# Streaming the rows of the projections' products backwards through TensorE

## The reference

```python
# first model, each of 2 layers, T = 272
proj = rms_norm(h, norm_mix_g[l]) @ w_in[l]                 # 1024 -> 2560
q, k, v, xr, gate = jnp.split(proj, splits, axis=-1)
h = h + jnp.concatenate([o_attn, o_rec], axis=-1) @ w_out[l]  # attention and a recurrence
g, u = jnp.split(rms_norm(h, norm_ffn_g[l]) @ w_gu[l], [D_FF], axis=-1)
h = h + (jax.nn.silu(g) * u) @ w_down[l]                    # 2816 -> 1024

# second model, each of 2 layers, T = 512 and 256
y, yc = even_mixer(xm, cm, w_in_ab, ...)  # layer 0: x @ w_in, gated MLP, windowed attention, @ w_out
y = odd_mixer(xm, cm, w_qkv_c, ...)       # layer 1: x @ w_qkv, attention, @ w_out
h = h + gt_m * rms_norm_2(y, g_post_m)
f = conv_ffn(modulate(h, ...), w_up[layer], conv_w[layer], conv_b[layer], w_down[layer])
h = h + gt_f * rms_norm_2(f, g_post_f)
```

## Time and profile before

| | |
|---|---|
| time, median of 3 runs | 1695.95 us (1694.21 to 1696.47) |
| the profiled execution | 1696.95 us |
| its span, first to last instruction | 1695.1 us |
| matmuls on TensorE | 11870, busy 1622.8 us (96%) |
| VectorE, ScalarE busy | 1017.2 us (60%), 869.4 us (51%) |
| moved by DMA | 253.94 MB, mean 150 GB/s |

### The profile page before, as it was taken

How to read it: one execution, slowest core, us unless ns; L and a number is a source line. 1 busy time by engine, 2 the same in 40 slices (tenths; PEclk the granted TensorE clock), 3 DMA queues, 4 the chain that set the end, 5 groups by cost and what they waited for, 6 DMA issues and landing times.

```text
span 1695.1 us, 28191 instructions
## 1 busy us (share of the span) xinstructions
PE 1622.8 (96%) x11870; PEld 1419.8 (84%) x11870; DVE 1017.2 (60%) x1577; ACT 869.4 (51%) x1467; POOL 21.1 (1%) x38
## 2 busy tenths in 40 slices
PE   6999999999999999999989999999999898999997
PEld 6968999989789999987757778888888674789997
DVE  7675545465756455724464765425556877687675
ACT  6764534448555444534565553323444647665563
POOL 0000000000000000310000000000000000000000
PEclk9999999999899999999999999999999999999999
DMA  7465445353556464772201553232223530254642
GB/s 297 140 248 210 159 156 200 138 193 139 199 190 233 141 232 142 208 242 82 75 1 56 182 207 104 84 126 100 84 69 112 207 114 26 76 217 150 218 145 91
DMA packets 60525, 253.94 MB, mean 150 GB/s; under 512 B 4977, under 2 KB 8305, under 8 KB 42481
## 3 DMA queue, kind: packets, MB, share of 16 engines
q1 hardware_dynamic: 59088, 249.01, 41.3%
q0 software_dynamic: 1312, 3.15, 1.0%
HBM read 251.09 MB, written 1.05 MB: 149 GB/s over the span
## 4 chain that ended last, share of the span: by engine, by line
PE 82%; DVE 9%; ACT 6%; issue 2%; DMA 0%; SPq 0%; DVEq 0%; ACTq 0%
PE PA L916 63%; PE PA L976 4%; DVE WL_t L1571 2%; PE PB L851 2%; PE PB L1339 2%; PE PA L1004 2%; ACT WH_t L2298 1%; PE PB L1326 1%; PE PA L953 1%; PE PA L958 1%; PE PA L952 1%; PE PA L871 1%; PE PB L1269 1%; ACT tmp L2741 1%; DVE Y L1953 1%
## 5 line engine op out<-in xcount | busy, mean ns | idle before, releaser
L916 PE MATMUL PA<-XH_t,WH_t 128*128 128x256 f32 (+2 forms) x1984 | 628.1, 317 | 3.7 <-DVE WL_t L1571 1.5
L1571 DVE TENSOR_TENSOR WL_t<-raw,WH_t 128x1024 fp32r<-128x1024 f32 (+1 forms) x344 | 444.5, 1297 | 307.2 <-ACT WH_t L2298 306.8
L916 PE MATMUL PA<-XL_t,WH_t 128*128 128x256 f32 (+2 forms) x1984 | 622.8, 314 | 0.0
L916 PE MATMUL PA<-XH_t,WL_t 128*128 128x256 f32 (+2 forms) x1984 | 622.6, 314 | 0.0
L2298 ACT ACTIVATE WH_t<-raw 128x1024 fp32r<-128x1024 f32 (+1 forms) x344 | 380.8, 1111 | 158.8 <-PE PA L916 139.6
L916 PEld LDWEIGHTS PA<-XH_t,WH_t 128*128 128x128 f32 x1984 | 375.8, 189 | 34.2 <-issue 6.0
L916 PEld LDWEIGHTS PA<-XH_t,WL_t 128*128 128x128 f32 x1984 | 375.8, 189 | 21.4
L916 PEld LDWEIGHTS PA<-XL_t,WH_t 128*128 128x128 f32 x1984 | 375.9, 189 | 21.3 <-issue 0.5
L916 PE MATMUL PA<-AH_t,WH_t 128*128 128x256 f32 (+2 forms) x616 | 192.0, 312 | 0.3 <-DVE AL_t L1617 0.2
L916 PE MATMUL PA<-AH_t,WL_t 128*128 128x256 f32 (+2 forms) x616 | 190.9, 310 | 0.0
L916 PE MATMUL PA<-AL_t,WH_t 128*128 128x256 f32 (+2 forms) x616 | 190.3, 309 | 0.0
(11 more groups left out here) (281 smaller groups left out, 1723.8 us busy)
## 6 DMA issues: line engine op xcount, KB each, us to landing
raw<-in_w_ada SPq DMA_DIRECT2D x48, 1024.0 KB, 5.0
raw<-in_w_gu SPq DMA_DIRECT2D x44, 1024.0 KB, 4.8
raw<-in_w_dn SPq DMA_DIRECT2D x64, 704.0 KB, 4.1
raw<-in_w_up SPq DMA_DIRECT2D x44, 1024.0 KB, 4.8
raw<-in_w_in SPq DMA_DIRECT2D x30, 1024.0 KB, 5.7
raw<-in_w_out SPq DMA_DIRECT2D x12, 1024.0 KB, 4.8
raw<-in_w_qkv SPq DMA_DIRECT2D x6, 1024.0 KB, 6.1
raw<-in_w_outc SPq DMA_DIRECT2D x4, 1024.0 KB, 4.8
```

What stands on the lines that cost most here:

```text
L916: mm = pe.matmul(PA[:, (L.b0 + o) % 4, 0:T], W[:, c:c + P], X[:, k, L.x0:L.x0 + T], start=(n == 0 and m == 0 and not L.early), stop=(n == ...
L1571: dve.tensor_tensor(WL_t[:, w:w + L.cols], RAWV[:, r % RAW, part * UNIT:part * UNIT + L.cols], WHf[:, w:w + L.cols], ALU.subtract).then_in ...
```

## The change

A helper `back` turns the order of columns of a view round: it starts at the last column and steps by -1. It is put around the PSUM operand and the moving operand of every product of the projections, at the five places named above. The same columns are multiplied and the same sums land in the same places; the order in which TensorE walks along a row is reversed. Weights, waits, signals, banks and the order of the products are as before.

```diff
+            def back(t):
+                return t[:, ::-1]
...
-                        pe.matmul(PA[:, (L.b0 + o) % 4, 0:L.T], W[:, c:c + P], X[:, k, L.x0:L.x0 + L.T],
+                        pe.matmul(back(PA[:, (L.b0 + o) % 4, 0:L.T]), W[:, c:c + P], back(X[:, k, L.x0:L.x0 + L.T]),
...
-                                mm = pe.matmul(PA[:, (L.b0 + o) % 4, 0:T], W[:, c:c + P], X[:, k, L.x0:L.x0 + T],
+                                mm = pe.matmul(back(PA[:, (L.b0 + o) % 4, 0:T]), W[:, c:c + P], back(X[:, k, L.x0:L.x0 + T]),
...
-                    pe.matmul(PA[:, bank, 0:L.T], WH_t[:, c:c + P], hi[:, k, 0:L.T], start=(k == 0), stop=False)
-                    pe.matmul(PA[:, bank, 0:L.T], WH_t[:, c:c + P], lo[:, k, 0:L.T], start=False, stop=False)
+                    pe.matmul(back(PA[:, bank, 0:L.T]), WH_t[:, c:c + P], back(hi[:, k, 0:L.T]), start=(k == 0), stop=False)
+                    pe.matmul(back(PA[:, bank, 0:L.T]), WH_t[:, c:c + P], back(lo[:, k, 0:L.T]), start=False, stop=False)
...
-                            pe.matmul(PA[:, bank % 4, a:b], WH_t[:, c:c + P], x[:, k, a:b], start=(k == 0 and x is hi),
+                            pe.matmul(back(PA[:, bank % 4, a:b]), WH_t[:, c:c + P], back(x[:, k, a:b]), start=(k == 0 and x is hi),
...
-                            mm = pe.matmul(PA[:, bank % 4, a:b], WL_t[:, c:c + P], hi[:, k, a:b], start=False,
+                            mm = pe.matmul(back(PA[:, bank % 4, a:b]), WL_t[:, c:c + P], back(hi[:, k, a:b]), start=False,
```

More of the change, by code:

```diff
@@ L957, in second_down @@
                     c = w + k * P
-                    mm = pe.matmul(PA[:, bank, 0:L.T], WL_t[:, c:c + P], hi[:, k, 0:L.T], start=False, stop=(k == FH - 1))
+                    mm = pe.matmul(back(PA[:, bank, 0:L.T]), WL_t[:, c:c + P], back(hi[:, k, 0:L.T]), start=False, stop=(k == FH - 1))
                 mm.then_inc(S("out_ready"), 1)
```

## The result

| | before | after |
|---|---|---|
| median of 4 runs | 1696.21 us (1694.21 to 1698.05) | 1704.34 us (1702.74 to 1704.61) |
| ratio to before | | 1.0047, 95% interval 1.0035 to 1.0059 |
| span of the profiled execution | 1695.1 us | 1702.8 us |

A forecast was written before the change was run, and what follows sets the result against it. PE's list of matmuls was taken to bound the kernel. With 0 per column, 0 per product and 0 elsewhere, the profiled 1696.95 us stayed, 1696.0 us against the median; the range was 1690 to 1724 us.

The forecast's parts named there:

- What bounds the kernel: Whole kernel: PE is busy 1622.8 of 1695.1 us; the touched 9024 products hold it for 1331 us, 78% of the span.
- Price per column, 0: Touched products, 2,906,880 columns: a backward step costs between 0 and +0.422 ns a column; 0 was taken.
- the half rate: Rival, touched products: a backward row loses the pairing of neighbours, +0.422 ns a column, 1227 us, giving 2924 us; chance 0.14.
- The two rows taken as evidence: L1021's moving row cut in runs of 64 and L1143's step-0 weight read: neither slower than ordinary, speaking for 0 per column.
- Same within 0.2%: Whole kernel: time changes by no more than about 3.4 us, following from the no-difference case; chance 0.72.
- The 0.72: Whole kernel: chance given to no difference, the likeliest case, at 1696.0 us.
- And their pattern isn't touched. So nothing outside the two patterns gets a price: Weight loads of 128 columns, 189 ns each, run under the products unchanged; everything outside the moving and PSUM patterns: 0 us.
- The split in 0.422 ns a column and 11.4 ns fixed: Touched products' pace, from 119.4 ns at 256 columns and 227.4 at 512: a cost per column plus a fixed part per product.
- The start cost: Rival, touched products: starting a backward row costs 1 to 3 ns each, 9 to 27 us, giving 1705 to 1724 us; chance 0.08.
- start on the same boundaries: Touched rows: seen from the other end, even widths and the 16-token offset keep neighbours paired, so cost per product was taken as 0.
- Less fixed cost: Rival, touched products: the fixed 11.4 ns shrinks by 1 ns (1688 us) up to all of it (1594 us); chance 0.06.
- PSUM: Sums in PSUM: each column is revisited after the same 119 to 227 ns and readers wait as before; 0 us.

## Why the prediction was right or wrong

**What bounds the kernel: right.** All of the 7.7 us appeared as busy time of PE; counts of products and columns held, and so did the leverage: 9.0 us for each nanosecond per product.

**Price per column, 0: right against the half rate, wrong as a form.** No product came near 0.84 ns a column; the upper end of 1227 us was not there. The two rows taken as evidence pointed the right way on that. But they are single means of few products, those of the earlier trace rows are durations with the way through the pipe and no paces, and they could not show 1 or 2%, which is the size of all that happened here (6.2 ns of 227.1). "Same within 0.2%" asked for a pace right to 0.4 ns per product, and no row of the trace bounds a change of the read pattern that tightly. The 0.72 was too high for that reason alone. That the time is within the range owes something to luck: 12.5 us lost at 512 columns and 5.7 us won at the other widths, by the ledger, stand behind the small sum, and the prediction had neither.

**"And their pattern isn't touched. So nothing outside the two patterns gets a price": this is the step that failed.** The weight loads run under the products and the chain never names them, yet a load's reads meet the row's. Moving the weights by 16 columns, with everything else as it was, took a 256-column product from 120.0 to 113.3 ns. The Trainium skill says in "TensorE: Matmul & The Clock Gate" (Step-by-step: what each phase is for) that PE has two read ports of its own, and that loading the next weights takes nothing from the running matmul's read bandwidth. The prediction priced the loads as if this held. The measured 6.7 ns speak against it for this pace, and they decide.

**The split in 0.422 ns a column and 11.4 ns fixed: a fit through two points, not a law.** Forwards the part beyond columns / 2.4 is 58 ns at 128 columns, 13.2 at 256, 10.0 at 264, 11.9 at 272, 13.3 at 384, 16.1 at 448. The check at 272 columns agreed within a nanosecond (126.2 against 126.7), but the effect in question is of that size, and the same kernel's other rhythm gives 125.3 there.

**The rivals.** The start cost forecast 1705 to 1724 us and the time came within a microsecond of it, but its mechanism is wrong: +6.2, -0.8 and -1.6 ns at three widths are no start cost. That the time lay near is no merit of that rival. (Its lower end is counted from the median and its upper from the profiled execution, 1 us apart.) The sentence that all rows "start on the same boundaries" looked at the row alone; the boundary that counts is the distance to the weights. "Less fixed cost" had the least chance, with no row for it, and came true in part: 272 columns and the 256 from XH did get faster.

**PSUM: right**, 0 us, and now measured alone.

## What to carry to other kernels

When one engine sets the time with thousands of equal instructions, ask of each edit what it does to a nanosecond of their pace, and give "no difference" only the chance that the rows can bear out at that size. Where fp32r products follow one another with a weight load each, the distance in SBUF between the weights and the moving rows, modulo 256 bytes, is worth a sweep: here it moved a 256-column product by 6% and the whole kernel by 0.5%, for two lines in the order of allotment. Which distance is best depends on the width (of those tried, 48 columns for 256 and 272, 0 for 512), so a kernel with several widths pays at one what it wins at another.

## What the runs showed of the hardware

- A product's pace depends on the distance between its row and the weights modulo 64 fp32 columns: 256 columns forwards took 120.0 ns at 0, 116.7 to 117.8 at 8, 113.3 or 117.8 at 16, 120.0 at 24, 113.3 at 48. Finer steps count too: a shift of the row by only 2 columns gave 126.3 ns.
- The pace isn't even from product to product: 256 columns backwards repeat 115, 119, 116, 123 ns, 512 columns forwards from AH 231, 226, 229. Only means over many products can be compared.
- The direction of the PSUM row changed nothing at any of ten widths from 128 to 512 columns beyond 0.2 ns.
- At 128 and at 192 columns the pace is 111.7 ns in every direction, so something other than the row sets it; the 110 ns of the earlier trace rows, with weight loads back to back, suggest the load.
- The same addresses and widths can run at more than one pace: 256 columns forwards at a distance of 16 went at 117.8 ns in two runs and at 113.3 in a third.
- Open: why 512 columns backwards stay at 233.3 ns at nearly every distance, and what picks the rhythm where the same addresses allow two.
